# Down-projection weights of chunks 1 to 8: the low part made by ScalarE and an adding transfer

## The reference, cut to what matters

```python
for layer in range(2):
    h = h + mix(rms_norm(h, norm_mix_g[layer]))
    hn = rms_norm(h, norm_ffn_g[layer])
    h = h + (silu(hn @ ffn_w_gate[layer]) * (hn @ ffn_w_up[layer])) @ ffn_w_down[layer]
return rms_norm(h, norm_final_g)
```

## Time and profile before

| | |
|---|---|
| median of 3 runs | 566.08 us (565.66 to 566.32) |
| the profiled execution | 566.0 us |
| its span, first to last instruction | 563.7 us |
| outside the span | 2.3 us |
| mean granted TensorE clock | 0.998 |
| DMA | 105.65 MB, mean 187 GB/s |
| mixer 0, FFN 0, mixer 1, FFN 1 | about 5 to 110, to 280, to 387, to 558 us |

### The profile page before, as it was taken

The page is one execution under the profiler, slowest core; times in us unless marked ns, Lnnn a source line. Parts: engine busy times, 40 slices in busy tenths (PEclk is TensorE's granted clock), DMA queues, the critical chain, the costliest instruction groups (busy, mean ns, idle before and its releaser), DMA issues.

```text
span 563.7 us, 7599 instructions
## 1 busy us (share of the span) xinstructions
PE 556.3 (99%) x2949; PEld 475.1 (84%) x2949; DVE 462.4 (82%) x571; ACT 324.7 (58%) x454; POOL 15.5 (3%) x55
## 2 busy tenths in 40 slices
PE   8999999999999999999999999999999999999995
PEld 7899978888888888888888888888888888888884
DVE  5679996786988869897796998977779888798875
ACT  6686864654564565555566356546475545555632
POOL 1200001000000000000000000000000000000000
PEclk9999999999999999999999999999999999999999
DMA  8984644465627384467479622445844464826421
GB/s 306 344 304 162 213 149 138 161 197 178 223 76 244 130 297 151 162 211 251 162 242 308 223 85 74 156 150 165 278 161 139 149 224 163 303 89 216 139 101 74
DMA packets 30420, 105.65 MB, mean 187 GB/s; under 512 B 3377, under 2 KB 4273, under 8 KB 30385
## 3 DMA queue, kind: packets, MB, share of 16 engines
q1 hardware_dynamic: 30240, 105.04, 55.0%
q10 hardware_dynamic: 144, 0.14, 0.1%
HBM read 104.11 MB, written 1.05 MB: 187 GB/s over the span
## 4 chain that ended last, share of the span: by engine, by line
PE 96%; DMA 1%; issue 1%; DVE 1%; SPq 0%; ACT 0%; POOLq 0%; POOL 0%; DVEq 0%
PE bank L1745 20%; PE bank L1747 20%; PE bank L1746 20%; PE bank L2178 13%; PE bank L2181 7%; PE bank L1843 4%; PE bank L1846 2%; PE bank L1790 1%; PE bank L1794 1%; PE bank L1797 1%; DMA raw<-in_slabs 1%; PE bank L1815 1%; PE bank L1935 1%; PE bank L2223 1%; PE bank L1961 0%
## 5 line engine op out<-in xcount | busy, mean ns | idle before, releaser
L1046 DVE TENSOR_TENSOR w_lo<-raw,w_hi 128x2048 fp32r<-128x2048 f32 (+2 forms) x92 | 204.7, 2229 | 32.7 <-ACT w_hi L574 32.7
L574 ACT ACTIVATE w_hi<-raw 128x2048 fp32r<-128x2048 f32 (+2 forms) x83 | 153.6, 1862 | 29.5 <-DMA raw<-in_slabs 27.3
L1745 PE MATMUL bank<-w_lo,yT_hi 128*128 128x512 f32 (+1 forms) x242 | 95.7, 396 | 0.0
L1747 PE MATMUL bank<-w_hi,yT_lo 128*128 128x512 f32 (+1 forms) x242 | 94.0, 388 | 0.0
L1746 PE MATMUL bank<-w_hi,yT_hi 128*128 128x512 f32 (+1 forms) x242 | 93.9, 388 | 0.0
L2178 PE MATMUL bank<-xT,w_hi 128*128 128x512 f32 x320 | 80.2, 392 | 0.0
L2178 PEld LDWEIGHTS bank<-xT,w_hi 128*128 128x128 f32 x320 | 58.0, 189 | 10.8
L1745 PE MATMUL bank<-w_lo,xT 128*128 128x512 f32 (+1 forms) x160 | 61.9, 387 | 0.0
L1747 PE MATMUL bank<-w_hi,xT 128*128 128x512 f32 (+1 forms) x160 | 60.8, 380 | 0.0
L1746 PE MATMUL bank<-w_hi,xT 128*128 128x512 f32 (+1 forms) x160 | 60.6, 379 | 0.0
L1747 PEld LDWEIGHTS bank<-w_hi,yT_lo 128*128 128x128 f32 x242 | 45.4, 188 | 9.6
(11 more groups left out here) (229 smaller groups left out, 838.4 us busy)
## 6 DMA issues: line engine op xcount, KB each, us to landing
raw<-in_slabs SPq DMA_DIRECT2D x170, 512.0 KB, 4.7
spare<-in_slabs SPq DMA_DIRECT2D x16, 512.0 KB, 5.1
raw<-in_slabs SPq DMA_DIRECT2D x6, 256.0 KB, 5.8
h<-in_x SPq DMA_DIRECT2D x2, 512.0 KB, 8.1
gain<-in_norm_ffn_g SPq DMA_DIRECT2D x2, 512.0 KB, 7.3
raw<-in_slabs SPq DMA_DIRECT2D x4, 128.0 KB, 5.3
h<-in_x_cols SPq DMA_DIRECT2D x1, 512.0 KB, 5.9
gain<-in_norm_mix_g SPq DMA_DIRECT2D x1, 512.0 KB, 6.7
```

The costliest lines, as they stand in the source:

```text
L574: A(w_hi[:, s % SLOTS, c], raw_of(r, c), ACT.Copy).then_inc(hi_ready, 1)
L1046: V.tensor_tensor(w_lo[:, s % SLOTS, c], raw_of(preps[s][0], c), w_hi[:, s % SLOTS, c].bitcast(F32), ALU.subtract).then_inc(lo_ready, 1)
L1745: T.matmul(o, st_hi, mv_lo, start=first, stop=False)
L1747: return T.matmul(o, st_lo, mv_hi, start=False, stop=last)
```

## The change

The down slabs of chunks 1 to 8 of both layers, 16 in all, are called far. For a far slab ScalarE makes the high part as before and then, from the same raw slab, a second copy with scale -1 into the slab's slot of `w_lo`, so that it holds minus the high part. It counts `neg_ready`. GpSimd waits for that count and issues one transfer of 1 MB that reads the slab from HBM again and adds it onto the slot of `w_lo`; when that has landed, the slot holds slab minus high part. VectorE does nothing for these slabs. TensorE waits on the transfer's semaphore (`far_lo`, one for each of the six slots), and on a smaller count of `lo_ready` for all others. SP waits on `neg_ready` before it reuses the raw slot or `spare`. GpSimd goes through the eight far slabs of a layer right behind its power for that layer's second FFN norm half.

```diff
+def is_far(key):
+    return key[0] == "down" and 1 <= key[2] <= NCH - 3
...
-        free[r] = [("lo", len(preps))]
+        if is_far(key):
+            far.append((len(preps) - 1, [k for k, *_ in loads].index(key)))
+            free[r] = [("neg", len(far))]
+        else:
+            free[r] = [("lo", len(preps) - len(far))]
+        near.append(len(preps) - len(far))
...
+        def lo_done(s):
+            return (far_lo[s % SLOTS], 16 * far_no(s)) if s in far_slabs else (lo_ready, near[s + 1])
...
+            def far_lows(l):
+                for n, (s, load) in enumerate(far):
+                    if loads[load][0][1] == l:
+                        pool.wait_ge(neg_ready, n + 1)
+                        nc.gpsimd.dma_start(w_lo[:, s % SLOTS, :], slabs[load], accum_op=ALU.add)\
+                            .then_inc(far_lo[s % SLOTS], 16)
...
                 nc.gpsimd.tensor_tensor(o, i, e, ALU.pow).then_inc(pow_done, 1)
+                if kind == "norm" and a % 2 and b == HALVES - 1:
+                    far_lows(a // 2)
...
                 A(w_hi[:, s % SLOTS, c], raw_of(r, c), ACT.Copy).then_inc(hi_ready, 1)
+                if s in far_slabs:
+                    A(w_lo[:, s % SLOTS, c], raw_of(r, c), ACT.Copy, scale=-1.0).then_inc(neg_ready, 1)
...
             def split_lo(s):
+                if s in far_slabs:
+                    return
...
-                pe.wait_ge(lo_ready, s + 1)
+                pe.wait_ge(*lo_done(s))
```

More of the change, by code:

```diff
@@ L76, in half_of_acts @@
     return (i + sum(i - 2 >= a for a in SEVEN_AT[l])) % 2
+def is_far(key):
+    return key[0] == "down" and 1 <= key[2] <= NCH - 3
 def places():
-    loads, preps, place = [], [], {}
+    loads, preps, place, far, near = [], [], {}, [], [0]
     ring, counts = list(range(RAW_SLOTS)), [0] * (RAW_SLOTS + 1)
@@ L140, in places @@
         place["end", l] = len(preps)
-    return loads, preps, place
+    return loads, preps, place, far, near
 QK_BANKS = ((0, 1), (4, 5), (4, 5))
@@ L170, in trunk @@
     assert SEQ == 2 * P and D == 1024 and DFF == NCH * 256 and POOL == 256 and CONV == 256
-    loads, preps, place = places()
+    loads, preps, place, far, near = places()
+    far_slabs = [s for s, _ in far]
     mix0 = [place["mix", l] for l in range(2)]
@@ L327, in trunk @@
         lo_ready = sem("lo_ready")
+        neg_ready = sem("neg_ready")
+        far_lo = [sem(f"far_lo{i}") for i in range(SLOTS)]
         slab_used = sem("slab_used")
@@ L400, in slot, with far_no @@
             return s % SLOTS
+        def far_no(s):
+            return sum(t % SLOTS == s % SLOTS for t in far_slabs if t <= s)
+        def lo_done(s):
+            return (far_lo[s % SLOTS], 16 * far_no(s)) if s in far_slabs else (lo_ready, near[s + 1])
         def raw_of(r, c=slice(0, SLAB)):
@@ L456, in load @@
                 for what, count in free or ():
-                    sp.wait_ge({"lo": lo_ready, "forms": forms_ready, "sum": block_sum}[what], count)
+                    sp.wait_ge({"lo": lo_ready, "neg": neg_ready, "forms": forms_ready, "sum": block_sum}[what], count)
                 for b in range(2):
@@ L1762, in unit @@
                     if k % per == 0:
-                        pe.wait_ge(lo_ready, s + k // per + 1)
+                        pe.wait_ge(*lo_done(s + k // per))
                     hi, lo = w_part(static + k // per, (k % per) * width, width)
@@ L1823, in qk_tile @@
                     if k % 4 == 0:
-                        pe.wait_ge(lo_ready, s + k // 4 + 1)
+                        pe.wait_ge(*lo_done(s + k // 4))
                     hi, lo = w_part(s + k // 4, (k % 4) * 512 + sub * P, P)
@@ L1835, in qk_pair_tile @@
                 b = QK_PAIR_BANKS[sub % 2]
-                pe.wait_ge(lo_ready, s + 2)
+                pe.wait_ge(*lo_done(s + 1))
                 if n < 2:
@@ L2265, in final_by_tiles @@
                     a_hi, a_lo = (t[:, half, 2 * LAST_ACT[l]:2 * LAST_ACT[l] + 2, :] for t in (actT_hi, actT_lo))
-                    pe.wait_ge(lo_ready, down_slab(l, e) + 1)
+                    pe.wait_ge(*lo_done(down_slab(l, e)))
                     for k in range(2):
```

## The result

The changed kernel takes 634.99 us (median of 4 runs, 633.03 to 638.05) and the one before 565.87 beside it: a ratio of 1.1225, interval 1.1207 to 1.1242, slower by 69 us. I forecast slower, with 605 and a range of 577 to 633. The sign came out, and so did the kind of cost, TensorE waiting for the transfer. The size did not: 69 us in place of 39, 2 us beyond the upper end.

A forecast was written before the change was run, and what follows sets the result against it. TensorE was taken to bound the kernel, so VectorE's relief gave 0. Waits for the transfer of 32.7 us, plus 10 for the clock, less 3.6 given back, made 39.1 on 566.0: 605 us, range 577 to 633.

The forecast's parts named there:

- What bounds the kernel: TensorE, busy 556.3 of 563.7 us; its 1.7 us of waits name no low part of a down slab.
- what the relief is worth: On VectorE, 16 subtractions of 2.29 us removed, 36.6 us, hidden behind products: 0 us off the path.
- Which slabs: TensorE's waits at slabs 3, 5, 4, 7, 8: 18.3 us in layer 0, 14.4 in layer 1; slabs 1, 2, 6 free.
- the time left: First use minus high part's end, second copy and lateness: 4.4 us at slab 3, 2.6 at slab 5, 8.2 at slab 4.
- L: Time from second copy's end to the adding transfer's landing: taken as 9 us, between bounds of 5.1 and 12.
- my own lines: Per-slab sum: wait is L less the time left, with slab 5 paying only what slab 3 has not; 32.7 us.
- The clock: On TensorE, half clock after five stalls over 4 us: 2 us each, 10 us; 3.6 us given back at slab 5.
- Loads: More DMA traffic, its share rising from about 55% to 65 or 70, may make loads later: 0 us.
- ScalarE's order: On ScalarE, 16 second copies of 1.9 us delay what stands behind: 1.1 us at slab 3, 3.0 at slab 5, 1.4 at slab 7.
- The long transfer: Rival: L of 12 us or more, with the neighbour load or a slow adder: 633 us; chance 0.18.
- The short one: Rival: short transfer, L between 5 and 7 us, since two reads may overlap: 577 to 590 us; chance 0.24.
- no slower: Rival: transfer hidden behind products, needing L of at most 2.6 us, or 4.0 without ScalarE's lateness: 566.0 us; chance 0.05.

The follow-up runs named there:

- Runs 7 and 8: Against the kernel before, only down slab 2 of each layer takes the new way (7), or only slab 1 (8): 566.06 us, ratio 1.0006; 565.86 us, ratio 1.0.
- run 3: The changed kernel with GpSimd's transfers plain, without accum_op, so they overwrite w_lo instead of adding: 602.05 us, ratio 1.0649.
- Runs 1 and 2: The changed kernel, with SP loading the next slab only after GpSimd's issue (1) or after the transfer's landing (2): 623.61 us, ratio 1.1023; 642.03 us, ratio 1.1356.
- Run 9: Against the kernel before, only down slab 7 of each layer takes the new way: 586.12 us, ratio 1.0355.
- run 4: The changed kernel, but VectorE adds the slab onto ScalarE's second copy and GpSimd does no transfer: 570.99 us, ratio 1.009.

## Why the prediction was off

**What bounds the kernel, and what the relief is worth.** Right. VectorE lost 34 us of work and no wait of TensorE was there for it to end. Runs 7 and 8, with two subtractions fewer each and no wait for a transfer, leave the time where it was.

**Which slabs.** Right for slabs 3 and 7, for slab 8 of layer 0 and for the ones that were to be free. Slab 4 was to wait 0.8 us and waited 4.5; slab 8 of layer 1 was to wait 0.8 and did not. Slab 5 was to wait 1.8 us less what the clock gives, and had none. At slab 3 of layer 0 the time left was 2.4 us, not 4.4, since its chain was late by a load.

**L, the step that failed.** "I take 9, between the ends and without the neighbour." Alone, the transfer takes 7.9 us from issue to landing, so the working for the bytes was good: 2.0 + 6.2 = 8.2, and run 3 shows the doubling by halving the packet. But it was not alone. The same count that starts it lets SP load the next slab, I had named this and priced it at 3.1 us for the upper end, and then left it out of the sum. SP's two issues end before GpSimd's one does, so loads are ahead of it every time but once. Measured, the median from second copy to last packet is 12.2 us; the landing comes some 0.3 us behind that. Put into my own lines for slabs 3, 4, 7 and 8, L = 12.2 gives 7.8, 4.0, 9.3 and 8.2 in layer 0 and 7.8, 4.0 and 9.6 in layer 1 (slab 8 of layer 1, at 7.9, is under its 8.2), 50.7 us, and with the 1.8 for each slab 5 it is 54.3. The seven waits make 54.1. That the totals meet so closely is partly luck. Slab by slab the lines give 7.8 where 10.0 and 10.1 were measured (slab 3), 4.0 for 4.5 and 4.4 (slab 4), 9.3 for 6.5 and 9.6 for 10.1 (slab 7), 8.2 for 8.5 (slab 8), and 1.8 for nothing (slab 5).

My sum was short by 31 us, 39.1 against 70.2. Of these 21.4 are waits (54.1 against 32.7), and 9.7 are the clock (16.1 against 10 less the 3.6 that I let it give back at slab 5). With L = 12.2 and 2 us at each of seven stalls my own steps give about 65 us.

**The clock.** I took 2 us at each of five stalls. Run 9 shows 2.0 at each of two. There were seven stalls over 4 us, so 14 us, and TensorE's products took 16.1 longer. Around slab 3 (PE, PEld, DVE, ACT, POOL busy, then the clock):

```profile
174.90:177.60 2.70, 0.05 (x1) 0.00 (x0) 2.70 (x2) 1.68 (x1) 0.00 (x0) 1.00 0.91 261
177.70:184.90 7.20, 0.00 (x0) 0.00 (x0) 7.13 (x7) 2.61 (x3) 0.00 (x0) 0.50 1.00 260
185.00:187.80 2.80, 2.80 (x7) 2.22 (x8) 1.70 (x2) 2.80 (x2) 0.00 (x0) 0.50 1.02 417
187.90:191.00 3.10, 3.10 (x15) 2.55 (x15) 0.00 (x0) 0.32 (x1) 0.87 (x1) 1.00 0.85 281
```

The clock was still full 2.7 us after the last product, was half for the rest of the wait and for the first 2.8 us of products behind it, and was full again then. The Trainium skill (TensorE: Matmul & The Clock Gate, Part 1) says that the array falls to half rate when idle and comes back only with sustained work; by that rule these stalls had to cost more than their length, and the trace agrees, with 2.8 us of products at half clock behind this one.

**Loads.** I took 0 us for them. In the changed kernel VectorE waited 8.7 us for loads before block sums, once on the way to slab 3 of layer 0. On the page's chain of work that ended last, loads into `raw` take 10% of the span, as much as the adding transfers, where they took 1% before. So the loads help to set when the second copies come. Runs 1 and 2 show what it costs to shield the transfer from them. How much of the 69 us goes to late loads alone wasn't separated, and stays open.

**ScalarE's order.** 1.1 to 3.0 us of lateness were in the sum; run 4 gives 5 us in all when nothing else is in the way.

**The rivals.** The long transfer, for which I gave 18 in 100 and 633 us, is what happened, by its neighbour, though its 633 had 10 us for the clock where 16 were measured. The short one would have needed neither adding nor neighbour. That it would be no slower was refuted by 7.9 us for the best of 16 transfers, against 2.6 to 4.4 us of time left at the tight slabs.

## What to carry to other kernels

Before work is moved to another engine, ask if the engine that ends last waits for it: here it did not, so the best outcome was no change (runs 7 and 8). When a transfer replaces an instruction of 2.3 us, compare its landing time with the time left at each use, and count the transfers that the same semaphore sets off: they run on the same engines, and here they turned 8 us into 12. A stall of several us has a price beyond its length, here some 2 us each, since the clock falls during it.

## What the runs showed of the hardware

- An adding transfer of 1 MB onto SBUF takes 7.9 us from issue to landing when alone, a plain one by the same way 5.0; its packets take 0.58 us against 0.30. The Trainium skill (DMA: Bandwidth & Descriptors, "Anatomy of one DMA") would give 4.4 for the plain one.
- With the issue of a 1 MB load begun 1.1 us before GpSimd's issue ends (slab 3 of layer 0), the first packet of the adding transfer starts 3.9 us after that end instead of 0.7. I had expected the two to share the engines from the start.
- GpSimd's issue of such a transfer takes 0.86 us when adding and 0.54 when plain.
